# The MLP of a diffusion trunk layer in two parts: all first products, then the second products of three rounds as seven half-size products

## What is computed

```python
h = layer_norm(x) * (1 + sc2) + sh2
ff = jnp.square(jax.nn.relu(h @ p['w_mlp1'] + p['b_mlp1'])) @ p['w_mlp2'] + p['b_mlp2']
x = layer_norm(ALPHA * x + g2 * ff, p['ln2_g'], p['ln2_b'])
```

## Time and profile before

| | us |
|---|---|
| median of 3 runs | 1562.36 (1561.36 to 1563.22) |
| the profiled execution | 1560.75, its span 1559.1 |
| PE busy in the span | 1502.1 (96%) |
| DVE busy | 1021.0 (65%) |
| ACT busy | 689.6 (44%) |
| POOL busy | 220.5 (14%) |

### The profile page before, as it was taken

How to read it: one execution, slowest core, us unless ns; L and a number is a source line. 1 busy time by engine, 2 the same in 40 slices (tenths; PEclk the granted TensorE clock), 3 DMA queues, 4 the chain that set the end, 5 groups by cost and what they waited for, 6 DMA issues and landing times.

```text
span 1559.1 us, 25181 instructions
## 1 busy us (share of the span) xinstructions
PE 1502.1 (96%) x10114; PEld 1394.2 (89%) x10114; DVE 1021.0 (65%) x1407; ACT 689.6 (44%) x1258; POOL 220.5 (14%) x230
## 2 busy tenths in 40 slices
PE   4999999999999989899999999999999999999997
PEld 2899999999999989898866799999998898998986
DVE  5666666658565688988876453346966773653768
ACT  2443343343564266777766443233532262451540
POOL 1011122100101100000000000000000541522720
PEclk9999999999999999999999999999999999999999
DMA  9555555543677777787630355335212122131241
GB/s 317 181 177 192 180 184 184 181 138 112 211 247 243 270 222 223 256 262 226 221 125 1 115 183 169 132 115 190 95 55 82 54 94 97 55 102 61 82 175 68
DMA packets 152511, 244.62 MB, mean 157 GB/s; under 512 B 8112, under 2 KB 110240, under 8 KB 149344
## 3 DMA queue, kind: packets, MB, share of 16 engines
q1 hardware_dynamic: 129232, 174.59, 33.5%
q0 software_dynamic: 12304, 47.72, 8.4%
q10 hardware_dynamic: 10880, 20.97, 5.2%
HBM read 196.63 MB, written 46.63 MB: 156 GB/s over the span
## 4 chain that ended last, share of the span: by engine, by line
PE 78%; DVE 13%; ACT 5%; DMA 1%; issue 1%; SPq 1%; ACTq 0%; DVEq 0%
PE acc L965 57%; PE tp L965 17%; ACT arena L1922 2%; DVE wlo L2288 1%; PE tp L1432 1%; DVE arena L2562 1%; DMA arena<-in_w_mod 1%; PE tp L1093 1%; DVE arena L2393 1%; ACT whi L1700 1%; DMA arena<-decay_sums_t 1%; DVE arena L2563 1%; ACT whi L2080 1%; DVE wlo L2763 1%; PE tp L1479 1%
## 5 line engine op out<-in xcount | busy, mean ns | idle before, releaser
L965 PE MATMUL acc<-hh,whi 128*128 128x322 f32 (+1 forms) x1068 | 287.0, 317 | 5.0 <-issue 3.0
L965 PE MATMUL acc<-hl,whi 128*128 128x322 f32 (+1 forms) x1068 | 280.6, 311 | 0.0
L965 PE MATMUL acc<-hh,wlo 128*128 128x322 f32 (+1 forms) x1068 | 279.9, 311 | 0.0
L965 PEld LDWEIGHTS acc<-hh,whi 128*128 128x128 f32 x1068 | 188.2, 189 | 9.7 <-issue 7.3
L965 PEld LDWEIGHTS acc<-hl,whi 128*128 128x128 f32 x1068 | 189.6, 189 | 0.0
L965 PEld LDWEIGHTS acc<-hh,wlo 128*128 128x128 f32 x1068 | 189.4, 189 | 0.0
L965 PE MATMUL acc<-whi,hh 128*128 128x256 f32 x640 | 183.1, 286 | 0.0
L965 PE MATMUL acc<-whi,hl 128*128 128x256 f32 x640 | 179.8, 281 | 0.0
L965 PE MATMUL acc<-wlo,hh 128*128 128x256 f32 x640 | 179.7, 281 | 0.0
L2288 DVE TENSOR_TENSOR wlo<-raw,whi 128x2048 fp32r<-128x2048 f32 x62 | 145.0, 2338 | 35.2 <-ACT whi L1700 35.2
L1700 ACT ACTIVATE whi<-raw 128x2048 fp32r<-128x2048 f32 x62 | 118.3, 1908 | 71.4 <-PE tp L965 48.3
(11 more groups left out here) (366 smaller groups left out, 3137.9 us busy)
## 6 DMA issues: line engine op xcount, KB each, us to landing
raw<-in_w_in SPq DMA_DIRECT2D x38, 1024.0 KB, 8.8
raw<-in_w_mlp SPq DMA_DIRECT2D x32, 1024.0 KB, 5.2
arena<-in_w_mod SPq DMA_DIRECT2D x24, 1024.0 KB, 8.3
arena<-decay_sums_t ACTq DMA_DIRECT2D x40, 512.0 KB, 6.0
arena<-xs_nat SPq DMA_DIRECT2D x8, 1024.0 KB, 10.7
raw<-in_w_ssd_o SPq DMA_DIRECT2D x8, 1024.0 KB, 6.6
y_nat<-arena POOLq DMA_DIRECT2D x6, 1024.0 KB, 7.5
arena<-y_nat SPq DMA_DIRECT2D x6, 1024.0 KB, 6.6
```

The source lines that it names most:

```text
L965: return pe.matmul(out, l, r, start=first, stop=last)
```

## The change

The MLP is worked off in two parts. **Part one**: the plain units of round 0 and then all twelve Strassen blocks. Each square (128 x 640) is written by ACT in place and stored to DRAM (`f_d`, 32 tiles); no halves are made of it here. DVE makes the sums of quadrants of h during the plain units.

**Part two**: second products of rounds 0 to 2 (`ff_round`), and then those of round 3 as before (`last_products`, with the tiles in the order 3, 4, 0, 1, 2). The squares of a round come back by one load of 2560 KB. The latents' 512 x 1024 by 1024 x 1024 product of a round is made by seven Strassen-Winograd products of 256 x 512 by 512 x 512 (24 matmuls of 512 columns each); the context tile is multiplied plainly by the four weight quadrants (48 matmuls). POOL makes the sums of quadrants: s1 to s4 of the squares and, in two halves each (a, b), t1 to t4 of the weights, every one 128x1024. Weights are halved in 16 pieces of 128x1024 a round (block e = 0 to 7, half h = 0 or 1), the squares' parts f0 to f6 and two context parts likewise. The seven products are summed over the three rounds in seven places and recombined once (`combined`). ACT goes through the same order as DVE below, without the evictions; it waits for POOL's sum of the block (t3 for e=2, t1 for e=3, t2 for e=4, t4 for e=6) or part (s3 for f1, s1 for f2, s2 for f3, s4 for f4), and for the bank or buffer to be free. x1, the residual, is stored whole and read back in two steps, its first three tiles only after `combined`.

The diff, cut to its core:

```diff
     with ExitStack() as ctx:
         def sb(n, shape, dt=F32):
...
+        SUMS = ("s3", "s1", "t1a", "t1b", "t3a", "t3b", "s2", "t2a", "t2b", "s4", "t4a", "t4b")
...
+
...
+            def ff_in(r):
+                for m in range(2):
+                    sp.wait_ge(s[f"f_out{m}"], 48 + 16 * HK * (r + 1))
+                sp.wait_ge(s["f_in"], 48 + 16 * r)
+                sp.dma_start(ff_whole(r), f_d[r * KT:(r + 1) * KT].rearrange("k p c -> p k c")).then_inc(s["f_in"], 16)
...
+                sp.wait_ge(lo["sem"], value(lo, 2))
+                if n < 2 * KT:
+                    load(n % 2, w_1[:, :, n * BW:(n + 1) * BW])
+                else:
+                    raw_in((0, ("b11", "b12")[n % 2]), quad(0, 0, n % 2))
+                if n == KT + 2:
+                    sp.wait_ge(s["x1_out"], LANDED + 16)
+                    raw_in((0, "b22"), quad(0, 1, 1))
+                    sp.wait_ge(s["t_ok"], LANDED + 4)
+                    ff_in(0)
+            sp.wait_ge(s["product"], A_END)
+            ff_in(1)
+            sp.dma_start(bias2, a["b_mlp2"][0, D // 2:].partition_broadcast(P)).then_inc(s["rows2_in"], 16)
+            for r in range(ROUNDS):
+                sp.wait_ge(lo["sem"], lo_due(r, 2, 1))
+                raw_in((r, "b21"), quad(r, 1, 0))
+                sp.wait_ge(s["ff_ok"], part_n(r, "f6"))
+                if r + 2 <= ROUNDS:
+                    ff_in(r + 2)
...
+                sp.wait_ge(lo["sem"], lo_due(r, 5, 1))
+                sp.wait_ge(s["sum_ok"], sum_n(r, "t2b"))
+                raw_in((r + 1, "b11" if r + 1 < ROUNDS else 0), quad(r + 1, 0, 0))
+                sp.wait_ge(lo["sem"], lo_due(r, 6, 1))
+                raw_in((r + 1, "b12" if r + 1 < ROUNDS else 1), quad(r + 1, 0, 1) if r + 1 < ROUNDS else quad(r + 1, 1, 0))
+                sp.wait_ge(lo["sem"], lo_due(r, 7, 1))
+                if r + 1 < ROUNDS:
+                    raw_in((r + 1, "b22"), quad(r + 1, 1, 1))
...
+                raw_in((ROUNDS, 2 + b), quad(ROUNDS, b, 1))
+            sp.wait_ge(s["x1_back"], 16)
+            sp.wait_ge(s["quad_out"], A_END + 1)
+            sp.dma_start(x1[:, 0:3], x1_d[0:3].rearrange("t p d -> p t d")).then_inc(s["x1_back"], 16)
...
+            def ff_sum(out, x, y, op):
+                po.tensor_tensor(out, x, y, op).then_inc(sums["sem"], step(sums))
+                po.wait_ge(sums["sem"], value(sums))
+
+            def weight_sum(r, first, dst, out, last):
+
+                for h in range(2):
+                    po.wait_ge(s["lo_done"], lo_due(r, dst, h))
+                    for key in last:
+                        po.wait_ge(*raw_due((r, key)))
+                    ff_sum(raw_half(out, h), raw_half(first, h), raw_half(out, h), ALU.subtract)
+
+            def round_begun(r):
+
+                po.wait_ge(s["f_in"], 48 + 16 * (r + 1))
+                if r:
+                    po.wait_ge(s["ff_ok"], part_n(r - 1, "f1"))
+                ff_sum(s3f, f11(r), f21(r), ALU.subtract)
+                ff_sum(f21(r), f21(r), f22(r), ALU.add)
+                x_, y_, z_ = ROLE[r]
+                weight_sum(r, y_, 0, x_, ("b12",))
+
+            po.wait_ge(s["product"], LANDED + 7 * (3 * S_BLOCKS - 1) + 3)
+            round_begun(0)
+            for r in range(ROUNDS):
+                x_, y_, z_ = ROLE[r]
+                weight_sum(r, z_, 1, y_, ("b22",))
+                po.wait_ge(s["ff_ok"], part_n(r, "f0"))
+                ff_sum(f11(r), f21(r), f11(r), ALU.subtract)
+                weight_sum(r, z_, 3, x_, ())
+                po.wait_ge(s["ff_ok"], part_n(r, "f3"))
+                ff_sum(f11(r), f12(r), f11(r), ALU.subtract)
+                weight_sum(r, y_, 4, x_, ("b21",))
+                if r + 1 < ROUNDS:
+                    round_begun(r + 1)
+
+            po.wait_ge(s["rows2_in"], 16 * 5)
+            po.wait_ge(s["x1_back"], 32)
+            po.wait_ge(s["quad_out"], A_END + 2)
+            po.tensor_tensor(xo[:, END], xo[:, END], g2r[:, 1], ALU.mult).then_inc(sums["sem"], step(sums))
+            po.tensor_scalar(x1[:, END], x1[:, END], ALPHA, None, ALU.mult).then_inc(sums["sem"], step(sums))
             po.wait_ge(sums["sem"], value(sums))
-            po.tensor_tensor(xo[:, t], xo[:, t], x1[:, t], ALU.add).then_inc(sums["sem"], step(sums))
+            po.tensor_tensor(xo[:, END], xo[:, END], x1[:, END], ALU.add).then_inc(sums["sem"], step(sums))
 
         @block.tensor
...
+            def ff_round(r):
+
+                for e in range(8):
+                    i = PRODUCT_OF[e]
+                    for h in range(2):
+                        pe.wait_ge(lo["sem"], lo_due(r, e, h))
+                        if h == 0 and i is not None:
+                            n = 7 * r + i
+                            pe.wait_ge(s["ff_ok"], part_n(r, f"f{i}"))
...
+                        if e in CTX_OF and h == 1:
+                            last = ctx_part()
+                        for u in range(2 if i is not None else 0):
+                            for k in range(2):
+                                kk = 2 * h + k
+                                fh_, fl_ = (part(n)[:, kk, u * P:(u + 1) * P] for part in (part_hi, part_lo))
+                                for m, w in ((fh_, wh), (fh_, wl), (fl_, wh)):
+                                    last = mul(pair_bank(n)[:, u], m, w[:, k], kk == 0 and m is fh_ and w is wh, kk == HK - 1 and m is fl_)
+                            if h == 1:
+                                last.then_inc(ready["sem"], step(ready))
+                        if e in CTX_OF and h == 0:
+                            last = ctx_part()
+                        if (e, h) in HALF_AT:
                             last.then_inc(half["sem"], step(half))
...
+            def kept_square(n, x):
+
+                act.activation(x, x, ACT.Square).then_inc(sq["sem"], step(sq))
+                act.wait_ge(sq["sem"], value(sq))
+                act.dma_start(f_d[n], x).then_inc(fout[n % 2]["sem"], step(fout[n % 2]))
...
+                    act.wait_ge(s["acc_free"], U_MLP + n + 1)
+                    kept_square(n, xb[:, n % 2])
                     step(ready)
+                    if n >= KT - 3:
+                        upper_sum(n - KT + 3)
...
+                            split_hi(n // 2 % 2)
+                        elif n == 5:
+                            step(raws[0])
+                            for i in range(4):
+                                upper_entry(i, 0)
+                        else:
+                            upper_sum(3)
+                            for i in range(4, 7):
+                                upper_entry(i, 0)
...
@@ -2216,59 +2396,120 @@
                 act.wait_ge(s["t_sum"], LANDED + n + 1)
                 act.activation(hi_, whole, ACT.Copy).then_inc(s["t_hi"], 1)
 
-            def second_splits(r):
-                if r == 0:
-                    for n in range(3):
-                        upper_sum(n)
-                act.wait_ge(half["sem"], due(half))
-                split_hi(0)
-                step(ready, NT)
-                act.wait_ge(ready["sem"], value(ready))
-                split_hi(1)
...
+            def lower_half(r, e, h):
+
+                g = 2 * e + h
+                dve.wait_ge(hi["sem"], due(hi))
+                dve.tensor_tensor(w_half(wlo, g), half_from(r, e, h), f32(w_half(whi, g)), ALU.subtract).then_inc(lo["sem"], step(lo))
...
+            def evicted(r, i):
+
+                n = 7 * r + i
...
+                    dve.wait_ge(ready["sem"], due(ready))
+                    whole, bank = SUM_OF[i][:, u], pair_bank(n)[:, u]
+                    if r == 0 and i < 4:
+                        ins = dve.tensor_copy(whole, bank)
+                    else:
+                        ins = dve.tensor_tensor(whole, whole, bank, ALU.add)
+                    ins.then_inc(free["sem"], step(free))
...
+            def ff_round(r):
+
+                lower_half(r, 1, 1)
+                lower_part(r, "ctx1")
+                lower_half(r, 2, 0)
+                evicted(r, 0)
+                lower_part(r, "f3")
+                for e, h in ((2, 1), (3, 0), (3, 1), (4, 0)):
+                    lower_half(r, e, h)
+                lower_part(r, "f5")
+                evicted(r, 1)
+                lower_half(r, 4, 1)
+                lower_half(r, 5, 0)
+                lower_part(r, "f4")
+                evicted(r, 2)
+                lower_half(r, 5, 1)
+                lower_part(r, "f6")
+                lower_half(r, 6, 0)
+                evicted(r, 3)
+                lower_half(r, 6, 1)
+                next_part(r + 1, 0)
+                lower_half(r, 7, 0)
+                evicted_ctx(1)
+                evicted(r, 4)
+                lower_half(r, 7, 1)
+                next_part(r + 1, 1)
+                next_part(r + 1, 2)
+                lower_half(r + 1, 0, 0)
+                evicted(r, 5)
+                lower_half(r + 1, 0, 1)
+                next_part(r + 1, 3)
```

(57 more changed lines are left out.)

479 lines of the change are left out of this document (301 added, 178 removed).

## The result

The changed kernel takes 1597.51 us (median of 4 runs, 1595.98 to 1598.39) beside 1562.18 us for the kernel before in the same comparison: ratio 1.0225, 95% interval 1.0207 to 1.0242. It is 2.2% slower. Its profiled execution has a span of 1594.3 us.

What follows compares the result with a forecast made beforehand. The prediction took the MLP as bound by TensorE's matmuls, with part two becoming bound by DVE and POOL taking turns. 1560.75 + 2.8 (start) + 20.4 (part two) + 4 (loads) + 4 (last stage) = 1592 us; range 1564 to 1606.

Steps and rivals of the forecast that it cites:

- PE's saving, 16.8 us: Second products: 216 matmuls of 512 columns a round instead of 240, 16.8 us less over three rounds.
- Start of part one, +2.8: After plain unit 7: Strassen product 1 waits for t2, made after unit 7; +2.8 us, bounds 0 and 5.
- A store lands before the buffer is written again: Strassen blocks: the squares' 320 KB store lands within 5.3 us, the buffer being rewritten about 7 us later; cost nothing.
- Part two, +20.4: Rounds 0 to 2: DVE's lowerings and POOL's sums take turns; 68 + 60 + 60 = 188 us against 167.7.
- The loop of 60 us: Part two, each round: DVE, POOL and ACT steps in written order take 60 us against PE's 50.3; bounds 54 and 63.
- Forecast of round 0, 68 us: Round 0: early s3, s1 and t1a delay the first lowerings, f4 at 45.7, giving 68 us; bound below 58.
- the two add up to nearly the round: Sign for part two: DVE's lowerings (1.8 us or more) and POOL's sums (3 us or more) together nearly fill the round.
- Loads, +4: Rounds 0 and 1: the squares' 2560 KB load on SP delays b11 for ACT; +4 us, range 0 to 16.
- Last stage, +4: MLP's end: POOL's three last-tile sums wait for x1 and take turns with DVE's tail; +4 us, bounds 0 and 8.
- (a): Rival, part two: POOL's sums fall into DVE's waits and evictions, PE stays the bound; 1553 us, chance 0.12.
- (b): Rival, part two: only the sum of port times binds, 54 us a round, without gaps; 1570 us, chance 0.2.
- (c): Rival, part two: squares' load at its slow end (12 more) or loop at 63 us; 1600 to 1612, chance 0.13.

Runs made afterwards that it cites:

- the run with tiny sums: Changed kernel with eleven of POOL's twelve sums of a round made on 8 columns (s3 whole; wrong operands): 1559.91 us.
- the run without it: Changed kernel with POOL's three sums of the last tile made on 8 columns instead of 1024: 1594.74 us, ratio 1.0219 to the kernel before.

## Why the prediction was right, point by point
**The time.** Forecast 1592, measured 1597.5, inside the forecast's own range of 1582 to 1599, and slower as forecast. The terms add to 31.2 and the spans differ by 35.2: 4.6 more at the start, 0.2 more in part two with the loads, 0.8 less at the end. The other 1.5 us are the median over the profiled execution (1595.98).

**PE's saving, 16.8 us.** Right in its price: the rounds of 50.2 us in the run with tiny sums are the 50.3 of the sum.

**Start of part one, +2.8; measured +7.35.** The chain was right (the wait is for the lower half of t2, L3223), its size was not. PE waited 6.1 us. I let unit 7's eviction start at 1178.89 as in the kernel before; it started at 1180.92, though PE had gone on from unit 7 to product 0 at 1177.95, because in DVE's order the sums of h's quadrants and the lowering of t3 stand ahead of it. Of the 3.3 us between the forecast 2.8 and the 6.1, 2.0 are this, 0.7 are that PE was through with product 0 at 1179.87 and not at 1180.6, and the rest lies between the steps. The move of those ten sums into the plain units was costed at nothing without naming what stands behind them. The other 1.8 us of PE's waits before round 0 are for evictions of plain units (L3182), behind the same sums. In the Strassen part PE had no wait after product 1, as forecast. One store did hold DVE up: in the last block it waited 2.66 us for a buffer, the store of 320 KB in it having taken 5.61 us where the median is 2.6. "A store lands before the buffer is written again" failed there. The chain of waits runs through this store:
```profile
1324.93 5.61 DMA ff_kept<-cst
...
1330.61 0.55 DVE cst L3269
```
Its price was not measured; it can't be more than the 2.66 us, and round 0 came out under its forecast all the same.

**Part two, +20.4; measured +24.6, with the loads' 4 in it +24.4.** Right in mechanism, and near in size: with the loads' own 6 taken out it is 18.6, beside 20.4. Its first cause, one claim that DVE's two-input instructions and POOL's sums pass between them, is shown by four runs: with POOL's sums nearly gone 1560 us, with POOL as busy but only writing 1567, with DVE's lowerings nearly gone 1565, with the sums on DVE 1570. The loop of 60 us measured 58.9 and 56.0 where the loads were out of the way; the second is below the 58 to 62 that the forecast gave itself, and what makes it shorter was not tested. Forecast of round 0, 68 us: measured 66.2. That the total of this part comes out to 0.2 us is luck: 1.8 too much for the rounds and 2 too little for the loads cancel. The Trainium skill, SBUF — State Buffer, section Who interferes with whom, has the claim as an exclusive lock, on which the later of the two instructions blocks fully; the timeline of round 0 above agrees, to the 1.1 us that a lowering needs once the sum has ended.

**The signs.** Most came as written: a mean of 1.81 for the lowerings and 3.02 for the sums, and PE waiting before block 2 in round 0 and, in the later rounds too, for (4,1) and f4. Three did not. PE was busy for 54 to 55 us of a round instead of 50, the rest being its lower clock, a term that the forecast had at nothing; as it lies off the chain, that did no harm. The prediction had PE waiting for lowerings alone, but 9.9 of its 28.9 us of waits are for the eviction of the first context product (L3317), which DVE's order puts behind the lowering of (1,0); it is the same lateness of DVE seen at another place. And "the two add up to nearly the round" was misworked: 23 x 1.8 + 12 x 3 is 77 already, because the time of a blocked instruction contains the other's. What comes near the round is the sum of the lone times, 54 of some 60.

**Loads, +4; measured 6.** The mechanism was right and the size was low: b11 took 11.35 and, in the second seam, 11.53 us behind the squares, just under the 11.7 to 17.7 given, and was issued 48.7 us into round 1 (1448.96 on the chain, by the windows' 1400.30), not 44.6, so that more of it stood out. Taking 4 "near the lower end" of 0 to 16 was the choice that failed, by 2 us.

**Last stage, +4; measured +3.2 against the kernel before, 3.8 by the windows of the run without it.** Right, by the named cause: the stretched instructions stand in the timeline beside POOL's sums.

**The rivals.** (a), PE stays the bound with the sums as they are, is excluded: it would have shown rounds of 50 us beside whole sums. (The 49 us of DVE that were to speak for it are 51 by the prediction's own prices, 1.36 x 29.4 + 11.0, before any overlap.) It is what the kernel becomes when the claim is taken apart, 1560 in the run with tiny sums against the 1553 worked out for it; the 7 us between are mostly the start (4.6) and the tail (1.8), mis-sized there as above. (b), only the sum of port times of 54 us, is excluded by 56.0 to 62.4. (c), loads at their slow end or a loop of 63, did not come: the loads landed at their fast end and cost 6 of its 16, and the loop without them was 56 to 59.

What stays open: no run held PE's waits and changed its clock. By the chain of waits, which holds no matmul from 1320.35 to 1499.44 and has the clock at 1.00 behind it, the 12.5 us of slower matmuls fall into time that PE would have waited anyway; that is read from one trace, not tried.

## What to carry to other kernels
Before moving matmuls' work into sums of operands, add up the lone times of DVE's instructions with two SBUF inputs and of POOL's that read SBUF, and compare the sum of both with PE's time, not each engine's busy time. Where it comes near (54 of 50.3 us here), give the sums to DVE itself: a sum of 128x1024 costs 1.13 us there and 2.4 us of the shared turn on POOL. Work of POOL that has to stay does no harm beside evictions from PSUM (0.68 us with and without it) or where it only writes; an order of this kernel built on that was not tried.

## What was new about the hardware
- A memset by POOL of 128x1024 f32 takes 0.955 us and neither slows DVE's subtractions (1220 ns in 52 instructions) nor is slowed by them. Of POOL's instructions here, those that read SBUF take turns with DVE's two-input ones.
- A small instruction waits like a large one: a DVE subtraction of 128x16 went from 0.17 to a mean of 0.82 us beside POOL's sums.
- The granted clock in part two is at one of its two levels: 0.50 for some microseconds after each wait of PE of 3.3 to 5.2 us, 1.00 after waits of 1.1 to 2.4 us and in rounds without a gap. Over a round it makes 0.92 to 0.95. The 12.5 us of slower matmuls cost nothing visible here, because DVE and POOL, and not PE, were what the rounds waited for.
